# Fewer filler products of TensorE in the norm chains of a Hyena and mLSTM backbone

## The chip, the cores and the metric

The kernel runs on one core of one Trainium2 chip. The metric is the device time of one execution in microseconds (us), as the median of several runs. The profile is of one execution.

## The reference, cut to what matters

The reference is a two-layer backbone over 256 context and 256 latent tokens with 1024 channels. Each layer is a SwiGLU feed-forward part (FFN), a token mixer (Hyena long convolution in layer 0, mLSTM in layer 1) and a second FFN. Each of these six parts starts from a normalised, scaled and shifted copy of the stream `h`, and a seventh norm gives the output:

```python
def rms_norm(x, g):
    y = xf * lax.rsqrt(jnp.mean(xf * xf, axis=-1, keepdims=True) + NORM_EPS)
    return y * g
def ada_pre(h, g, shift, scale):
    return rms_norm(h, g) * (1.0 + scale) + shift
...
h_lat = h_lat + 0.5 * m_lat[2] * swiglu(ada_pre(h_lat, norm_g[l, 0], m_lat[0], m_lat[1]), ...)
h_lat = h_lat + m_lat[5] * y_lat
...
return rms_norm(h_lat, final_g)
```

What is computed does not depend on the products that the change leaves out: nothing reads their result.

## The kernel before, in words

`h` lies in SBUF as eight tiles of 128 channels by 512 tokens. Weights come in 172 blocks of 1 MB through two buffers. ScalarE (ACT) makes the rounded copy `w_hi` (L414), VectorE (DVE) the rest `w_lo` (L807, in two halves in L816), and TensorE (PE) takes each product of a weight and an activation as three products, `w_hi*act_hi`, `w_hi*act_lo` and `w_lo*act_hi` (L1436 to L1438, and L1465 to L1479 in the first two blocks after a norm, `in_pair`). Semaphores order all of it; each engine's program is written out by hand. `w_used` counts weight blocks that TensorE has finished with.

Each of the output projections 0 to 5 (`out_proj`) ends in a call of `chain(o + 1, cols)`: the norm chain. I number the chains 1 to 6. Chains 1 to 4 have all 512 tokens, chains 5 and 6 the 256 latent ones alone; chain 6 is the final norm. A chain runs across three engines:

- TensorE ends the last block. DVE adds each tile of the projection to `h` (L1004), ACT squares it (L425, L428), DVE adds up the squares (L922).
- TensorE sums the squares over the channels with products of one column (`square_sums`, L1514).
- ACT takes the root (L437), DVE the reciprocal (L876) and spreads it on a diagonal (L878).
- TensorE spreads the diagonal over all partitions with one product by ones (`rms_rows`, L1540).
- DVE scales tile by tile (L909), ACT shifts and rounds it to `act_hi` (L449), DVE makes `act_lo` (L895), and TensorE starts `in_pair` (L1465) as soon as the first tile is there. In chain 6 DVE writes the output instead (L902), and two DMAs store it.

While TensorE waits for these steps it is given filler products: `keep_warm(bank, n)` issues n products of the constant tile `cond_pad` with itself, 32 by 256 results in fp32, into a PSUM bank that is free (L1429). In the trace each such product stands as two matmul records. Chain 1 has one filler and otherwise uses the time for real products (`skip_rows`, L1547). Chains 2 to 6 have seven fillers each: three ahead of the sums of squares, two after them, two after the product by ones. The last of the first three (in chain 1 the only one) carries the increment of `w_used` for the last block of the projection; ACT waits for it before it makes `w_hi` of the second block after the norm. The wait for `h_ready` at the head of `chain` makes sure that bank 5 has been read before a filler writes it.

There are 20 more fillers ahead of chain 1 (L1655 to L1713). They are not touched.

Of the kernel before, what the change touches and what calls it, by code (L numbers as in the profile page):

```python
# [73 lines left out]
def build(nc, dram):  # L74
    at, n_vec = column_places()
    with ExitStack() as ctx:
# [12 lines left out]
        def sem(name):  # L89
            return ctx.enter_context(nc.semaphore(name))  # L90
# [112 lines left out]
        w_hi_done, w_lo_done, w_used = sem("w_hi_done"), sem("w_lo_done"), sem("w_used")  # L203
# [1220 lines left out]
        def _(pe):  # L1424
            def keep_warm(bank, n):


                for _ in range(n):
                    mm = pe.matmul(ps[0:32, bank, 0:256], cond_pad[:, 0, :],  # L1429
                                   cond_pad[:].rearrange("p k c -> p (k c)"), start=True, stop=True)  # L1430
                return mm
# [76 lines left out]
            def square_sums(n, cols):  # L1508

                w = (cols.stop - cols.start) // P  # L1510

                def column(t, x, start):
                    c = slice(cols.start + t * P, cols.start + t * P + P)
                    return pe.matmul(ss_col(n, t, 1), x[:, c], col("mean_w"), start=start, stop=not start)  # L1514

                for t in range(w):
                    if w == 4 and t == 0:
                        pe.wait_ge(sq_half, n)
                    elif t == w - 2:
                        pe.wait_ge(sq_ready, 8 * n)  # L1520
                    column(t, sq[:, 1], True)
                pe.wait_ge(sq_added, 6 * n)
                for t in range(w):
                    mm = column(t, sq_sum, False)
                mm.then_inc(ss_done, 1)
# [10 lines left out]
            def rms_rows(n, cols):  # L1536

                pe.wait_ge(diag_ready, n + 1)
                w = (cols.stop - cols.start) // P
                pe.matmul(ps[:, rb_bank(n), cols], ones[:], diag[:, 0:w, :], start=True, stop=True).then_inc(rb_ready, 1)  # L1540

            def skip_rows(u):

                if u == 0:
                    pe.wait_ge(f_dve, DVE_F["skip"])
                for ct in range(4):
                    mm = pe.matmul(ps[:, SKIP_BANKS[u], ct * P:ct * P + P],  # L1547
                                   col("hy_skip", 4 * u + ct).to_broadcast([P, P]), ident[:], start=True, stop=True)
                mm.then_inc(k_skip, 1)

            def chain(n, cols):

                pe.wait_ge(h_ready, 8 * n + 6)
                if n == 1:
                    keep_warm(5, 1).then_inc(w_used, 1)
                    skip_rows(0)
                else:
                    keep_warm(5, 3).then_inc(w_used, 1)
                square_sums(n, cols)
                if n == 1:  # L1560
                    skip_rows(1)
                else:
                    keep_warm(7, 2)
                rms_rows(n, cols)
                if n == 1:
                    skip_rows(2)
                else:
                    keep_warm(7, 2)

            def ffn_in(f, n, cols):  # L1570
                g0 = G_FFN[f]
# [20 lines left out]
            def out_proj(o, cols, between=None):  # L1592
# [53 lines left out]
                for m in range(KT):  # L1646
                    for k in range(2):
                        w, x = ops(k, m)
                        mm = product(ps[:, m, cols], w, x, False, k == 1)
                    mm.then_inc(y_done, 1)  # L1650
                chain(o + 1, cols)


# [449 lines left out]
```

## Time and profile before

| what | us |
|---|---|
| median of 3 runs | 2000.35 |
| the three runs | 1996.58, 2000.86, 2000.35 |
| the profiled execution's own time | 1996.49 |
| its span, first to last instruction | 1994.7 |
| TensorE busy in the span | 1945.8 (98%) |
| VectorE busy | 1214.9 (61%) |
| ScalarE busy | 660.6 (33%) |
| mean granted TensorE clock | 0.987 of full |

The profiled execution's time is its span and 1.8 us around it. A row of the windows view gives a stretch in us from the start of the span, its length, busy time of an engine with its number of instructions, the granted TensorE clock in it (1.00 is 2.4 GHz, 0.50 is 1.2 GHz), the share of time that the DMA engines were busy, and GB/s. A row of the timeline gives start, busy length, engine, line, operation and count, and in square brackets how long the engine was idle before it and what ended that.

### The profile page before, as it was taken

What the parts mean: (1) busy time and instruction counts of PE and PEld (TensorE: products, weight loads), DVE (VectorE), ACT (ScalarE), POOL (GpSimd) and SP (SyncE); (2) the same over time, 40 slices, a digit from 0 to 9 for tenths busy, and PEclk for the clock granted to TensorE, in tenths of its full rate; (3) what the DMA queues carried; (4) which work ended last, traced back from release to release, by engine and by line L of the source; (5) the groups of instructions that cost most, each with busy time, mean ns of one, the idle gap of its engine ahead of it and who ended that gap; (6) DMA issues with size and microseconds to landing.
All of it is one profiled execution on the core that took longest, in us unless ns stands there. A gap on an engine that the chain in (4) does not pass through costs nothing.

```text
span 1994.7 us, 25029 instructions
## 1 busy us (share of the span) xinstructions
PE 1945.8 (98%) x9586; PEld 1583.6 (79%) x9586; DVE 1214.9 (61%) x1608; ACT 660.6 (33%) x679; POOL 85.4 (4%) x169
## 2 busy tenths in 40 slices
PE   8999999999989999999999999999999999899998
PEld 3688888887867778888888788888877768499998
DVE  6976776567568757766755977233273346765455
ACT  5622222243231143221223422222243346444333
POOL 0000100000000000001000010000000010000000
PEclk9899999999999999999999999999999999999999
DMA  9355555422230015555543365222312213044543
GB/s 344 143 188 185 200 186 183 146 86 85 89 116 1 34 64 190 181 197 199 181 157 116 127 201 190 93 105 85 139 64 79 80 64 128 22 140 177 189 174 121
DMA packets 48321, 271.64 MB, mean 136 GB/s; under 512 B 5380, under 2 KB 6148, under 8 KB 24840
## 3 DMA queue, kind: packets, MB, share of 16 engines
q1 hardware_dynamic: 28536, 194.30, 27.5%
q0 software_dynamic: 19728, 76.55, 11.5%
q8 instruction: 39, 0.64, 0.1%
q14 instruction: 18, 0.15, 0.0%
HBM read 269.79 MB, written 1.05 MB: 136 GB/s over the span
## 4 chain that ended last, share of the span: by engine, by line
PE 92%; DVE 5%; ACT 2%; issue 1%; DMA 0%; DVEq 0%; ACTq 0%; SPq 0%
PE ps L1436 25%; PE ps L1437 25%; PE ps L1438 25%; PE ps L1763 2%; PE ps L1844 1%; PE ps L1465 1%; PE ps L1753 1%; PE ps L1466 1%; PE ps L1471 1%; PE ps L1468 1%; PE ps L1929 1%; PE ps L1806 1%; PE ps L1429 1%; PE ps L1479 1%; PE ps L1475 1%
## 5 line engine op out<-in xcount | busy, mean ns | idle before, releaser
L1436 PE MATMUL ps<-act_hi,w_hi 128*128 128x512 f32 (+1 forms) x2560 | 922.0, 360 | 11.0 <-DVE w_lo L807 6.7
L1437 PE MATMUL ps<-act_lo,w_hi 128*128 128x512 f32 (+1 forms) x2560 | 918.7, 359 | 0.0
L1438 PE MATMUL ps<-act_hi,w_lo 128*128 128x512 f32 (+1 forms) x2560 | 918.3, 359 | 0.0
L807 DVE TENSOR_TENSOR w_lo<-w_raw,w_hi 128x2048 fp32r<-128x2048 f32 x167 | 382.6, 2291 | 481.0 <-ACT w_hi L414 480.9
L1436 PEld LDWEIGHTS ps<-act_hi,w_hi 128*128 128x128 f32 x2560 | 485.7, 190 | 87.1 <-DVE w_lo L807 7.5
L1437 PEld LDWEIGHTS ps<-act_lo,w_hi 128*128 128x128 f32 x2560 | 485.9, 190 | 70.7 <-issue 0.5
L1438 PEld LDWEIGHTS ps<-act_hi,w_lo 128*128 128x128 f32 x2560 | 485.8, 190 | 70.6
L414 ACT ACTIVATE w_hi<-w_raw 128x2048 fp32r<-128x2048 f32 x172 | 329.1, 1913 | 620.6 <-PE ps L1438 597.5
L834 DVE SCALAR_TENSOR_TENSOR ada_w<-ada_w,cond_bc 128x1024 f32<-128x1024 f32 x128 | 156.2, 1221 | 0.0
L834 DVE SCALAR_TENSOR_TENSOR ada_prod<-ada_w,cond_bc 128x1024 f32<-128x1024 f32 x128 | 156.1, 1220 | 0.0
L463 ACT ACTIVATE silu_g<-ps 128x1024 f32<-128x1024 f32 (+1 forms) x44 | 40.4, 919 | 295.3 <-PE ps L1438 295.3
L383 POOL DMA_DIRECT2D ada_w<-ada_rows_dram x126 | 66.5, 528 | 1111.0 <-DVE ada_w L834 1106.6
L938 DVE TENSOR_TENSOR scratch<-silu_g,ps 128x1024 f32 (+3 forms) x44 | 47.8, 1087 | 65.2 <-PE ps L1438 65.2
L1763 PE MATMUL ps<-dft_i,zf 128*128 128x256 f32 x256 | 60.8, 398 | 7.3 <-DVE zf L1222 6.8
L1763 PEld LDWEIGHTS ps<-dft_i,zf 128*128 128x128 f32 x256 | 51.1, 201 | 19.1 <-DVE zf L1222 8.0
L1148 DVE TENSOR_SCALAR xc<-pad,vec 128x512 f32<-128x512 f32 x16 | 9.3, 582 | 75.4 <-ACT pad L665 75.4
L1004 DVE SCALAR_TENSOR_TENSOR h<-ps,coef_g,h 128x256 f32<-128x256 f32 x80 | 35.6, 478 | 32.2 <-PE ps L1438 32.2
L964 DVE TENSOR_TENSOR act_lo<-scratch,act_hi 128x1024 fp32r<-128x1024 f32 (+1 forms) x48 | 52.5, 1096 | 1.7 <-ACT act_hi L497 1.7
L497 ACT ACTIVATE act_hi<-scratch 128x1024 fp32r (+3 forms) x48 | 45.2, 945 | 16.5 <-DVE scratch L1233 11.7
L449 ACT ACTIVATE act_hi<-tn,mods 128x256 fp32r<-128x256 f32 x88 | 39.8, 502 | 32.2 <-DVE tn L909 32.2
L625 ACT ACTIVATE pad<-ps,vec 128x512 f32<-128x512 f32 x24 | 15.3, 685 | 95.0 <-PE ps L1438 85.3
L895 DVE SCALAR_TENSOR_TENSOR act_lo<-tn,mods,act_hi 128x256 fp32r<-128x256 f32 x88 | 38.9, 480 | 2.6 <-ACT act_hi L449 2.6
(231 smaller groups left out, 1336.8 us busy)
## 6 DMA issues: line engine op xcount, KB each, us to landing
w_raw<-w_stream_dram SPq DMA_DIRECT2D x172, 1024.0 KB, 4.7
ada_w<-ada_rows_dram POOLq DMA_DIRECT2D x128, 512.0 KB, 3.8
ada_raw<-ada_stream_dram POOLq DMA_DIRECT2D x4, 1024.0 KB, 12.4
ada_in<-ada_stream_dram POOLq DMA_DIRECT2D x4, 1024.0 KB, 16.3
bd<-bd_dram SPq DMA_DIRECT2D x4, 768.0 KB, 6.6
edecay<-log_decay_dram SPq DMA_DIRECT2D x4, 512.0 KB, 10.3
h<-tokens_dram SPq DMA_DIRECT2D x1, 2048.0 KB, 13.0
wg<-wg_dram SPq DMA_DIRECT2D x3, 512.0 KB, 4.5
```

Of the source, the lines that this page charges most:

```text
L383: pool.dma_start(ada_w[:, s], dram["ada_rows"][bass.ds(2 * q + s, 1)].rearrange("a p k -> (a p) k")).then_inc(adaw_loaded[s], 16)
L414: act.activation(w_hi[:, g % 2, :], w_raw[:, g % 2, :], ACT.Copy).then_inc(w_hi_done, 1)
L463: act.activation(silu_g[:, :, cols], ps[:, 0:2, cols], ACT.Silu).then_inc(silu_done, 1)
L497: act.activation(act_hi[:, s:s + 2, cols], src(b, i), ACT.Copy).then_inc(in_hi, 1)
L807: dve.tensor_tensor(w_lo[:, g % 2, :], w_raw[:, g % 2, :], w_hi[:, g % 2, :].bitcast(F32), ALU.subtract).then_inc(w_lo_done, 1)
L834: dve.scalar_tensor_tensor(ada_w[:, s] if cd else ada_prod[:], ada_w[:, s], 1.0, cond_bc[:, cd], ALU.mult, ALU.mult, accum_out=mod_cols[:, ...
L938: dve.tensor_tensor(hidden[:, bass.ds(2 * p + 2 * i, 2), cols], silu_g[:, :, cols], ps[:, 2:4, cols], ALU.mult).then_inc(mul_done, 1)
L964: dve.tensor_tensor(act_lo[:, s:s + 2, cols], src(b, i), act_hi[:, s:s + 2, cols].bitcast(F32), ALU.subtract).then_inc(in_lo, 1)
L1436: pe.matmul(out, wh, xh, start=start, stop=False)
L1437: pe.matmul(out, wh, xl, start=False, stop=False)
L1438: return pe.matmul(out, wl, xh, start=False, stop=stop)
L1763: mm = pe.matmul(ps[:, inv_bank(st) + ct // 2, ct % 2 * 256:ct % 2 * 256 + 256], zf[:, (st + 1) % 2, q, ct * P:ct * P + P], dft_i[:, q // ...
```

## The change

Chains 2 to 6 keep one filler of seven: the one that carries the increment of `w_used`. It is issued as the first now, where it was the third. Chain 1 and all fillers ahead of it stay. The order of all other instructions, and all waits, stay.

```diff
                     keep_warm(5, 1).then_inc(w_used, 1)
                     skip_rows(0)
                 else:
-                    keep_warm(5, 3).then_inc(w_used, 1)
+                    keep_warm(5, 1).then_inc(w_used, 1)
                 square_sums(n, cols)
                 if n == 1:
                     skip_rows(1)
-                else:
-                    keep_warm(7, 2)
                 rms_rows(n, cols)
                 if n == 1:
                     skip_rows(2)
-                else:
-                    keep_warm(7, 2)
```

## Rows read from the trace of the kernel before

**Rows 1.** The page: chain that ended last by engine; costliest group of instructions.

```profile
PE 92%; DVE 5%; ACT 2%; issue 1%; DMA 0%; DVEq 0%; ACTq 0%; SPq 0%
L1436 PE MATMUL ps<-act_hi,w_hi 128*128 128x512 f32 (+1 forms) x2560 | 922.0, 360 | 11.0 <-DVE w_lo L807 6.7
```

**Rows 2.** View of line L1429: count: min/median/max ns, first and last start.

```profile
L1429 PE MATMUL ps<-cond_pad x112: 379/379/636, 4.3 to 1989.0; 128*32 128x256 f32 x112
```

**Rows 3.** Timeline of chain 2, its last DVE update of `h` to `in_pair`.

```profile
733.16 1.48 PE L1429 MATMUL ps<-cond_pad 128*32 128x256 f32 x6
...
733.99 0.42 ACT L425 ACTIVATE sq<-h 128x256 f32<-128x256 f32 x1 [0.36 <-DVE h L1004]
...
734.58 1.05 PE L1514 MATMUL ps<-vec,sq 128*128 128x1 f32 x8
...
736.45 1.05 PE L1429 MATMUL ps<-cond_pad 128*32 128x256 f32 x4
...
736.72 1.90 ACT L414 ACTIVATE w_hi<-w_raw 128x2048 fp32r<-128x2048 f32 x1
...
737.07 0.69 DVE L878 TENSOR_TENSOR diag<-ident,cols 128x512 f32<-128x512 f32 x1
...
737.82 1.12 PE L1540 MATMUL ps<-diag,ones 128*128 128x512 f32 x2 [0.31 <-DVE diag L878]
...
738.87 1.05 PE L1429 MATMUL ps<-cond_pad 128*32 128x256 f32 x4
738.98 1.65 DVE L909 SCALAR_TENSOR_TENSOR tn<-h,coef_a,ps 128x256 f32<-128x256 f32 x4
...
741.00 0.47 PE L1465 MATMUL ps<-act_hi,w_hi 128*128 128x512 f32 x1 [1.08 <-ACT act_hi L449]
```

**Rows 4.** Windows of TensorE over chains 1 (four), 2, 5 and 6.

```profile
434.00:435.50 1.50, 1.50 (x11) 1.00 0.00 0
435.50:438.90 3.40, 3.10 (x27) 1.00 0.00 0
439.00:442.30 3.30, 3.22 (x10) 0.50 0.37 97
442.50:446.00 3.50, 3.43 (x15) 1.00 0.45 190
733.10:741.00 7.90, 6.51 (x34) 1.00 0.10 17
...
1787.20:1793.10 5.90, 5.27 (x27) 1.00 0.00 0
1984.20:1989.40 5.20, 5.11 (x25) 1.00 0.01 2
```

**Rows 5.** The chain that ended last, around chain 2: start, us, what.

```profile
733.24 1.41 PE ps L1429 x6
734.65 1.89 PE ps L1514 x16
```

**Rows 6.** Timeline of chain 6: its product by ones, its last fillers, the output.

```profile
1987.66 0.70 PE L1540 MATMUL ps<-diag,ones 128*128 128x256 f32 x2
...
1988.29 1.05 PE L1429 MATMUL ps<-cond_pad 128*32 128x256 f32 x4
1988.40 3.22 DVE L902 SCALAR_TENSOR_TENSOR out_sb<-h,vec,ps 128x256 f32<-128x256 f32 x8 [0.79 <-PE ps L1540]
```

**Rows 7.** Timeline of chain 1 on TensorE, cut to four rows.

```profile
434.00 0.62 PE L1429 MATMUL ps<-cond_pad 128*32 128x256 f32 x2
...
438.68 1.83 PE L1540 MATMUL ps<-diag,ones 128*128 128x512 f32 x2 [0.30 <-DVE diag L878]
...
440.31 1.91 PE L1547 MATMUL ps<-ident,vec 128*128 128x128 f32 x8
...
442.57 0.47 PE L1465 MATMUL ps<-act_hi,w_hi 128*128 128x512 f32 x1 [0.35 <-ACT act_hi L449]
```

**Rows 8.** Windows of TensorE around two other gaps, at 476 and at 1734 us.

```profile
476.40:479.90 3.50, 0.00 (x1) 1.00 0.00 0
479.95:486.70 6.75, 6.15 (x15) 0.50 0.44 155
486.80:493.55 6.75, 6.75 (x32) 1.00 0.45 155
...
1734.56:1737.80 3.24, 0.00 (x1) 1.00 0.00 0
```

**Rows 9.** Waits of TensorE from 1793 to 1830 us: who, for whom, total, times, longest.

```profile
PE ps L1436 <- DVE w_lo L807: 0.6, 1, 0.6
```

## The prediction, made before the changed kernel ran

> **What bounds the kernel now.** I read the page first. The chain of work that ended last is 92% TensorE, and the costliest group alone is 922.0 us of products [rows 1]. So almost every microsecond in which TensorE does its weight products more slowly is a microsecond of the end time. The fillers stand with 112 records in the view of their line [rows 2]. Each product is two records, so that is 56 products: 20 ahead of chain 1, 1 in chain 1, 35 in chains 2 to 6. The change removes six in each of five chains: 30 products, 60 records.
>
> Next I read the timeline of one chain [rows 3]. The reader should see that TensorE waits three times there: for squares from ACT, for the diagonal from DVE, and for the first `act_hi` tile. The fillers lie in these waits. Then I read the windows for the granted clock [rows 4]: over the whole of chains 2, 5 and 6 it is 1.00, and in chain 1, which has one filler, it falls to 0.50 from 439.0 to 442.3 us. Chains 3 and 4 repeat chain 2 within 0.1 us, also at 1.00. The question of this change is what the clock does once the fillers are gone.
>
> **The change part by part.**
>
> *Time of the fillers themselves: 0.* Removing work from a wait gives nothing back if something else ends the wait. Ahead of the sums of squares, L425 on ACT ends at 733.99 + 0.42 = 734.41 and L1514 starts at 734.58; in that time the fillers (733.16 for 1.48 us) are just draining [rows 3]. The chain view puts them on the path, with 1.41 us [rows 5], because they stand just ahead on the engine. If that were right, leaving out two of three would give 2/3 of 1.41 = 0.94 us in each of five chains, 4.7 us in all. I take 0, because the start fits the end of L425. The two fillers after the sums end at 736.45 + 1.05 = 737.50, and the product by ones starts at 737.82, after the diagonal (737.07 + 0.69 = 737.76). The last two end at 739.92, and `in_pair` starts at 741.00, on `act_hi`. In chain 6 the last two run beside the output, which DVE had already begun to wait for [rows 6]. All 0.
>
> *The earlier increment of `w_used`: 0.* Two fillers less ahead of it bring it about 0.9 us earlier. Only ACT's L414 waits for it there, and in program order L414 stands behind the root. It starts at 736.72, two microseconds after the increment has come [rows 3]; what hides it is the root. No queue is passed, and no wait is added.
>
> *The clock.* Chain 1 shows what happens with one filler. From 434.0 to 438.9 us TensorE ran one filler, 16 records of L1547 and 16 of one-column products; it was busy 1.50 + 3.10 of 4.90 us, and at 439.0 the clock was 0.50 [rows 4]. After the change chains 2 to 6 have over the same steps one filler and the one-column products alone: less than a chain that fell. So I expect all of them to fall. Chain 1 also shows the way back: after the product by ones it still had eight records of L1547, 1.91 us [rows 7], which kept TensorE busy (3.22 of 3.30 us) at the low clock, and at 442.5 the clock was 1.00 again, in time for `in_pair`. Chains 2 to 5 have nothing there. TensorE is idle from the end of the product by ones, 737.82 + 1.12 = 738.94, to 741.00 [rows 3], and it must win the clock back with the weight products themselves, at half speed.
>
> *The price, bounded from both sides.* The lower end is chain 1. Its product by ones took 1.83 us instead of 1.12, which is 0.71 us on the path [rows 3, 7]. The whole chain from the first filler to `in_pair` took 442.57 - 434.00 = 8.57 us against 741.00 - 733.16 = 7.84, so 0.73: the same. The upper end adds a gap that was followed by dense products: after the gap at 476 us the clock was 0.50 from 479.95 to 486.7, in which TensorE was busy 6.15 us [rows 8]. The row behind it has 32 records in the same 6.75 us against 15, so half of the 6.15 us is lost: 3.1 us. Both together are 3.8 us for a chain. If all is unknown, a gain is excluded: a lower clock makes nothing faster. Where between 0.7 and 3.8 a chain lands depends on when in the chain the clock falls and comes back, which differs from chain to chain. The case is nearer to the second row, as the recovery is by dense products, but not all of the low stretch need lie behind the start of `in_pair`, and not every product by ones need fall in it. I take the middle, 2.25 us, for chains 2, 3 and 4: 6.75 us.
>
> *Chain 5* has half as many tokens; its product by ones is 0.70 us, as the one of chain 6 [rows 6], so at half clock I add 0.4. The dense part costs up to 3.1, and TensorE later waits 0.6 us for `w_lo` [rows 9], which a slower start would hide. So 0 + 0.4 to 0.4 + 3.1 - 0.6 = 2.9 us, and I take the middle, 1.6. *Chain 6* has no dense products behind it, and its product by ones, at 1987.66, comes only 3.5 us after its first filler [rows 4, 6], so it is often still at the full clock: 0 to 0.4, I take 0.1. After chains 2 to 4 no wait of TensorE stands that could hide the loss.
>
> *The sum* is 6.75 + 1.6 + 0.1 = 8.4 us. Against the profiled execution's 1996.49 that makes 2004.9. That execution lies 3.9 us below the median of the runs shown; the four times known (1996.49, 1996.58, 2000.35, 2000.86) have a mean of 1998.6, and a median of new runs should lie about 8.4 above that: **2007.0 us**.
>
> A rule that speaks for another sum: here a chain in which TensorE was never idle for more than 0.35 us fell [rows 4, 7], while 3.24 us without a product at 1734.56 left the clock at 1.00 [rows 8]. The Trainium skill, in "TensorE: Matmul & The Clock Gate", section "HAM oscillation — how this bites in real kernels", ties the fall to gaps in which TensorE is idle. By that rule the changed chains, whose longest idle time is shorter than the gap at 1734.56, would hold the clock, and the sum would be 0. By the rows it is 8.4, since chain 1 contradicts the rule.
>
> **The rivals.**
>
> *The clock holds (0.09): not slower.* The mechanism is idle time and not the kind of work. Its place is TensorE's longest idle time after the change, 738.94 to 741.00, which is 2.06 us. For it speaks that the gap of 3.24 us at 1734.56 cost no clock; against it, chain 1. It decides if idle times of about 2 us do not bring the fall. The rule of the Trainium skill named above is this mechanism. Sum 0: time 1996.5 to 2000.9, within 0.2%. Should it hold in some chains only, the sum shrinks by 2.25 for each.
>
> *The clock falls but is back before `in_pair` (0.05).* Each chain would then cost what chain 1 cost: 3 x 0.7 + 0.4 = 2.5 us, so 2001.1. Against it: with no product between 738.94 and 741.00 nothing shows TensorE busy there.
>
> *The fillers were on the path (0.04).* The chain view says so [rows 5]; the clock would have to hold too. Price: a gain of up to 4.7 us, 1994. Against it stands the end of L425 just ahead of L1514 [rows 3].
>
> *The forecast (0.82):* at least three of chains 2 to 5 fall and come back only behind the start of `in_pair`.
>
> **How the numbers follow.** The four chains fall independently, so their ends do not all meet: I take 5 to 12 us for the sum rather than 2.1 to 14.7. With a low base of 1996.5 and a high one of 2000.4 the range is 2001.5 to 2012. It leaves out the rivals (0.18 together, of which the second reaches its edge) and little else. What a measurement of this kernel can tell from no change is about 0.2%, 4 us. Slower by more than that: nearly all of the forecast, 0.78. Within it: the clock that holds, the early recovery, and the small end of the forecast, 0.17. Faster: 0.05.
>
> **What would show each step.** Right: the windows of chains 2 to 5 show a granted clock of 0.50 from somewhere in the chain to 2 to 6 us behind the start of `in_pair`; weight products there stand 0.43 us apart instead of 0.23; some products by ones take about 1.8 us; L425 to L1514 and the diagonal to L1540 keep their distances; the mean clock falls from 0.987 by about 0.005. Wrong: a clock of 1.00 through chains 2 to 5, or L1514 starting earlier after the last block than now, or a wait on `w_lo` later in the FFN that shrinks by as much as the clock costs.

## The result, and where the time went

The changed kernel takes 2012.19 us as the median of 7 runs (2006.18 to 2016.23), the kernel before 2000.86 (7 runs, 1996.58 to 2005.03). The ratio is 1.0058, with a 95% interval of 1.0044 to 1.0072: by it the change costs 11.6 us, between 8.8 and 14.4 (the two medians lie 11.3 apart). The profiled execution took 2014.09 us, its span is 2012.2 and its mean granted clock 0.975, against 0.987.

The profile page of the changed kernel shows nearly the same busy times as before. The chain that ended last has 90% TensorE instead of 92, and the costliest group, L1436, is at 922.1 us instead of 922.0 [rows 1]. A part of the loss shows in the smaller group L1465, the first weight products behind a chain:

```profile
L1465 PE MATMUL ps<-act_hi,w_hi 128*128 128x512 f32 (+1 forms) x96 | 39.8, 417 | 8.6 <-ACT act_hi L449 8.6
```

Before, its mean was 379 ns, and it waited 4.1 us for `act_hi`. The page does not say where that happens. The windows of TensorE over the chains do. The columns are those of [rows 4].

```profile
738.74:740.80 2.06, 1.95 (x16) 1.00 0.00 0
740.83:746.10 5.27, 2.08 (x2) 0.50 0.36 110
746.11:751.07 4.96, 4.96 (x12) 0.50 0.23 96
751.10:756.00 4.90, 4.90 (x23) 1.00 0.00 0
...
1112.90:1116.20 3.30, 1.32 (x2) 0.50 0.40 112
1116.28:1119.70 3.42, 3.42 (x8) 0.50 0.45 192
...
1485.79:1491.70 5.91, 5.91 (x14) 0.50 0.18 72
...
1808.26:1812.60 4.34, 4.34 (x20) 0.50 0.58 236
```

The first four are chain 2: the sums of squares still run at 1.00, the product by ones at 0.50, and `in_pair` starts at 746.11 and does twelve records in 4.96 us at 0.50, where the same length at 1.00 holds 23. The others are chain 3, and the first products of `in_pair` after chains 4 and 5. Before, none of these stretches was below 1.00: chains 2, 5 and 6 are in [rows 4], chains 3 and 4 stood at 1.00 too, and these are the windows behind chains 2 to 5 in the kernel before:

```profile
741.00:751.00 10.00, 10.00 (x44) 1.00 0.22 93
1108.30:1119.70 11.40, 11.37 (x50) 1.00 0.19 80
1475.40:1491.70 16.30, 16.30 (x72) 1.00 0.22 78
1793.10:1812.00 18.90, 18.32 (x151) 1.00 0.51 175
```

After the change the weight products run at the low clock for 4.96, 3.42, 5.91 and 4.34 us, and about half of this is lost. From the fall to the return the low clock lasts about 10.2 us in chains 2 and 4 and about 6.8 us in chains 3 and 5:

```profile
740.85:751.05 10.20, 7.02 (x14) 0.50 0.30 104
1112.90:1119.70 6.80, 4.74 (x10) 0.50 0.43 154
1481.55:1491.75 10.20, 8.03 (x16) 0.50 0.28 104
1805.80:1812.60 6.80, 5.54 (x22) 0.50 0.41 155
```

The timeline of chain 3 has the steps of [rows 3]:

```profile
1107.96 0.62 PE L1429 MATMUL ps<-cond_pad 128*32 128x256 f32 x2
...
1108.78 0.42 ACT L425 ACTIVATE sq<-h 128x256 f32<-128x256 f32 x1 [0.36 <-DVE h L1004]
...
1109.25 1.05 PE L1514 MATMUL ps<-vec,sq 128*128 128x1 f32 x8 [0.67 <-ACT sq L425]
...
1112.49 1.73 PE L1540 MATMUL ps<-diag,ones 128*128 128x512 f32 x2 [1.29 <-DVE diag L878]
...
1114.26 1.66 DVE L909 SCALAR_TENSOR_TENSOR tn<-h,coef_a,ps 128x256 f32<-128x256 f32 x4 [0.69 <-PE ps L1540]
...
1116.28 0.77 PE L1465 MATMUL ps<-act_hi,w_hi 128*128 128x512 f32 x1 [2.06 <-ACT act_hi L449]
```

The product by ones takes 1.73 us instead of 1.12, and DVE now waits for it. In chains 2 and 4 TensorE is busy with it for 2.08 and 2.07 us. To give each chain one price I take, from the timelines, the time from the start of the last weight product ahead of the chain (L1438) to the start of the last product of `in_pair` (L1479); in chain 6 it ends at the start of the first output (L902). Before, these are 29.77, 29.79, 29.81, 17.50 and 4.43 us.

| chain | 2 | 3 | 4 | 5 | 6 | sum |
|---|---|---|---|---|---|---|
| added by the change, us | 3.16 | 2.10 | 3.62 | 2.17 | 0.48 | 11.5 |
| predicted | 2.25 | 2.25 | 2.25 | 1.6 | 0.1 | 8.4 |

The two chains with the longer low stretch cost most. The sum of 11.5 us is as much as the measured difference. This one profile is 17.6 us longer than that of before; the other 6 us lie elsewhere, and 4.4 of them ahead of chain 1 (its last weight product starts at 438.11 instead of 433.68), where both kernels have the same program.

One profile is one execution, and stretches that the change does not touch can go either way. Chain 1, whose program is the same in all the kernels of this document, fell to 0.50 before [rows 4] and held the clock in the changed kernel's profile:

```profile
441.00:446.20 5.20, 3.83 (x26) 1.00 0.15 32
```

Over the nine profiles taken for this document it fell in five and held in four. For the chains with one filler or with all seven there was no such doubt: chains 2 to 6 fell in both profiles of the changed kernel, ten of ten, and held, ten of ten, in the two kernels that keep all seven (before, and `more_gaps` below).

### The profile page after: what moved, and what is told of

It reads as the page before. It is cut to its first block, busy times and chain, and to the rows that moved or that the text cites. A ratio compares the mean times of both kernels' runs of the same rounds, so it can differ in the third digit from the quotient of the medians.

```text
span 2012.2 us, 24909 instructions
## 1 busy us (share of the span) xinstructions
PE 1948.7 (97%) x9526; PEld 1588.1 (79%) x9526; DVE 1214.6 (60%) x1608; ACT 660.7 (33%) x679; POOL 85.4 (4%) x169
## 3 DMA queue, kind: packets, MB, share of 16 engines
q0 software_dynamic: 19728, 76.55, 11.3%
HBM read 269.79 MB, written 1.05 MB: 135 GB/s over the span
## 4 chain that ended last, share of the span: by engine, by line
PE 90%; DVE 6%; ACT 2%; issue 1%; DMA 0%; DVEq 0%; ACTq 0%; SPq 0%
PE ps L1436 24%; PE ps L1438 24%; PE ps L1437 24%; PE ps L1759 2%; PE ps L1840 1%; PE ps L1465 1%; PE ps L1466 1%; PE ps L1749 1%; PE ps L1468 1%; PE ps L1471 1%; PE ps L1925 1%; PE ps L1802 1%; PE ps L1475 1%; PE ps L1479 1%; PE ps L1679 1%
## 5 line engine op out<-in xcount | busy, mean ns | idle before, releaser
L1436 PE MATMUL ps<-act_hi,w_hi 128*128 128x512 f32 (+1 forms) x2560 | 922.1, 360 | 11.0 <-DVE w_lo L807 6.7
L1438 PE MATMUL ps<-act_hi,w_lo 128*128 128x512 f32 (+1 forms) x2560 | 918.9, 359 | 0.0
L1436 PEld LDWEIGHTS ps<-act_hi,w_hi 128*128 128x128 f32 x2560 | 486.3, 190 | 86.6 <-DVE w_lo L807 7.5
L1438 PEld LDWEIGHTS ps<-act_hi,w_lo 128*128 128x128 f32 x2560 | 486.1, 190 | 71.0
L414 ACT ACTIVATE w_hi<-w_raw 128x2048 fp32r<-128x2048 f32 x172 | 329.1, 1913 | 626.1 <-PE ps L1438 597.6
L1465 PE MATMUL ps<-act_hi,w_hi 128*128 128x512 f32 (+1 forms) x96 | 39.8, 417 | 8.6 <-ACT act_hi L449 8.6
```

What stands on the lines that cost most here:

```text
L414: act.activation(w_hi[:, g % 2, :], w_raw[:, g % 2, :], ACT.Copy).then_inc(w_hi_done, 1)
L1436: pe.matmul(out, wh, xh, start=start, stop=False)
L1438: return pe.matmul(out, wl, xh, start=False, stop=stop)
L1465: pe.matmul(ps[:, t, cols], wh[0][:, k, c[t]], act_hi[:, k, cols], start=k == 0, stop=False)
```

## The experiments

I set two theories against each other. **A**: the clock falls in these chains because too few products of many columns are left in them, whatever the busy time says. **B** is that it falls because TensorE is idle in the waits. That is the rule of the Trainium skill, "TensorE: Matmul & The Clock Gate", section "HAM oscillation — how this bites in real kernels". All kernels but `more_gaps` differ from the changed kernel in the fillers of chains 2 to 6 alone, if at all. In the diffs, lines of chain 1 and bare `else:` lines are left out.

**Busy, but narrow.** `narrow` issues products of one column:

```diff
+            def narrow(bank, n):
+                for _ in range(n):
+                    pe.matmul(ps[:, bank, 0:1], ident[:], col("mean_w"), start=True, stop=True)
...
                     keep_warm(5, 1).then_inc(w_used, 1)
+                    narrow(5, 4)
                 square_sums(n, cols)
+                    narrow(7, 4)
                 rms_rows(n, cols)
+                    narrow(7, 4)
```

> The changed kernel, with each filler of 256 columns that it left out replaced by two products of one column with 128x128 weights, about the same busy time (some 0.48 us against 0.43). Theory A (the clock is held by products that stream many columns, whatever the busy time says): the granted clock falls to 0.50 in chains 2 to 5 as in the changed kernel, and the time is 8 to 14 us above the kernel before. Theory B (the clock falls because TensorE is idle in the waits): its longest idle time in a chain is now as short as before the change, the clock stays at 1.00 in chains 2 to 5, and the time is within 2 us of before.

Measured: 2011.9 us (4 runs), ratio 1.0055 [1.0037, 1.0074]: 11 us slower, just as the changed kernel. Chain 2 on TensorE, first as timeline and then in windows (the helper moves the lines: L1436 is the narrow filler, L1519 the sums, L1545 the product by ones, L1470 the first weight product):

```profile
737.44 0.62 PE L1429 MATMUL ps<-cond_pad 128*32 128x256 f32 x2
737.99 1.05 PE L1436 MATMUL ps<-vec,ident 128*128 128x1 f32 x8
738.90 1.03 PE L1519 MATMUL ps<-vec,sq 128*128 128x1 f32 x8
739.79 1.03 PE L1519 MATMUL ps<-vec,sq_sum 128*128 128x1 f32 x8
740.69 1.75 PE L1436 MATMUL ps<-vec,ident 128*128 128x1 f32 x8
742.30 2.05 PE L1545 MATMUL ps<-diag,ones 128*128 128x512 f32 x2
744.14 1.71 PE L1436 MATMUL ps<-vec,ident 128*128 128x1 f32 x8
746.41 0.76 PE L1470 MATMUL ps<-act_hi,w_hi 128*128 128x512 f32 x1 [0.56 <-ACT act_hi L449]
```

```profile
737.00:740.80 3.80, 3.80 (x31) 1.00 0.00 0
740.90:746.40 5.50, 4.95 (x18) 0.50 0.34 113
746.41:751.00 4.59, 4.59 (x11) 0.50 0.21 89
```

TensorE is busy for 3.80 of 3.80 us and the clock falls all the same. Its longest idle time in the chain is 0.56 us, shorter than the 1.08 us with which the kernel before kept the clock [rows 3]. That settles it against B, if idle means that no product is under way. The clock fell in chains 3 to 6 too. Chains 2 to 5 add 3.3, 3.9, 2.3 and 2.3 us by the measure of the table. For A it shows that the narrow products did not do the work of the wide ones. The two kinds differ in more than their columns, though: a filler has 32 columns of weights and other data, a narrow product has 128. Which of this counts was not tested.

**Which fillers matter.** Four kernels give back some of the groups; I name them by the fillers in the three places. Before is 3, 2, 2; the changed kernel is 1, 0, 0.

```diff
-                    keep_warm(5, 1).then_inc(w_used, 1)
+                    keep_warm(5, 3).then_inc(w_used, 1)
```

is `first_only` (3, 0, 0). The others put `keep_warm(7, 2)` back ahead of `rms_rows` (`middle_only`: 1, 2, 0), behind it (`last_only`: 1, 0, 2) or at both (`one_two_two`: 1, 2, 2).

> Three fillers ahead of the sums of squares, none behind them. Theory A: from the sums to the first weight product, 6.4 us, there is only the product by ones, so the clock falls in chains 2 to 5 nearly as in the changed kernel: 7 to 12 us above before. Theory B: the idle times of 1.3 and 2.06 us behind the sums stay as they were, so also 7 to 12 us. It tells where the fillers matter, not why.

> One filler ahead of the sums, two between the sums and the product by ones, none behind it. Theory A: the stretch without wide products is cut in two, and the second fillers join the product by ones; the clock falls in some chains only, 1 to 7 us above before. Theory B: the idle time of 2.06 us ahead of the first weight product is the longest and stays, so the time is that of the changed kernel, 8 to 14 us above.

> One filler ahead of the sums, none between, two behind the product by ones. Theory A: the clock falls as in the changed kernel around the sums, but the last fillers keep TensorE busy at half clock up to the first weight product, as L1547 does in chain 1, and bring the clock back sooner: per chain 0.7 to 2 us instead of 2 to 3.6, in all 3 to 7 us above before. Theory B: the longest idle time is now 1.3 us, nearly the 1.08 of before, so the clock holds and the time is within 2 us.

> Only the two fillers ahead of the sums of squares are left out, those behind stay: 10 of the 30. Theory A: the stretch without a wide product is 734.6 less some 0.9 us earlier to 736.4, not much longer than before; the clock holds in most chains, 0 to 2 us above before, and L1514 starts 0.1 us earlier after the last weight product, as in the changed kernel. If each filler counts the same, 10 of 30 give a third of 11.6 us: about 4 us above.

| fillers | median, us | ratio to before | chains 2 to 5, added in the profile, us |
|---|---|---|---|
| 1, 0, 0 | 2012.19 | 1.0058 [1.0044, 1.0072] | 3.2, 2.1, 3.6, 2.2 |
| 3, 0, 0 | 2007.36 | 1.0032 [1.0022, 1.0043] | 2.8, 2.2, 2.2, 2.2 |
| 1, 2, 0 | 2007.95 | 1.0034 [1.0020, 1.0047] | 2.8, 1.5, 1.5, 2.1 |
| 1, 0, 2 | 2003.16 | 1.0013 [1.0002, 1.0024] | 1.6, 1.4, 1.5, 1.0 |
| 1, 2, 2 | 2002.63 | 1.0012 [1.0003, 1.0022] | 1.1, 1.0, 0.8, 1.0 |

(The median of before beside them is 2000.86 for the first, 2001.41 for the next three and 2000.61 for the last.) The chains of the one profile add more than the medians differ, by 1 to 3 us in the last four rows. What sets this off elsewhere is open, so I compare these kernels by their medians and use the profiles for the mechanism.

`first_only` came out at 6.4 us [4.4, 8.6], under its 7 to 12 but for the end of the interval. `middle_only`, with 6.8 us [4.0, 9.4], is within A's 1 to 7 and just under B's 8 to 14, and its interval reaches into both, so it does not decide. A's mechanism was not right there either: I expected a fall in some chains only, and the clock fell in each of chains 2 to 5, in chain 2 twice. In chains 3 and 4 it fell only behind the start of `in_pair`, and they paid less (1.5 us). `last_only`, with 2.6 us [0.4, 4.8], lies under A's 3 to 7, and its time alone would not exclude B; its windows do:

```profile
736.80:740.40 3.60, 2.91 (x20) 1.00 0.00 0
740.50:745.70 5.20, 3.92 (x6) 0.50 0.28 95
745.80:747.30 1.50, 1.50 (x4) 0.50 0.82 344
747.40:751.00 3.60, 3.60 (x18) 1.00 0.00 0
```

The clock falls in chain 2 (as in 3 to 5), but only 1.5 us of weight products run at the low level, instead of 4.96. The last fillers don't keep the clock here; with them it comes back sooner. That is what I expected of them, with a smaller remainder. In `one_two_two` I was wrong on the mechanism: I expected the clock to hold in most chains, and it fell in each of chains 2 to 5. Its chain 2:

```profile
738.60:742.20 3.60, 2.93 (x21) 1.00 0.00 0
742.40:745.70 3.30, 3.30 (x6) 0.50 0.00 0
745.80:748.00 2.20, 1.12 (x6) 1.00 0.80 309
747.94:751.00 3.06, 3.06 (x14) 1.00 0.28 115
```

It is back at 1.00 before the first weight product at 747.94, so that the chain pays for its product by ones and no more. Chains 3 and 4 do the same. This is the prediction's second rival, at somewhat more than its price (0.8 to 1.1 us a chain instead of 0.7), in another kernel. Chain 5 still runs its first weight products low. So the two fillers ahead of the sums are worth 2.4 us [0.6, 4.4], though they save no wait. Between `last_only` and `one_two_two`, which differ in the middle fillers, the medians show no difference that counts (2.6 and 2.4 us above before).

**The changed kernel once more.**

> The changed kernel once more, for a second profile. Theory A: the clock falls in chains 2 to 5 again, but elsewhere in each chain and for other lengths, so that a chain costs 2 to 4 us with another distribution over the chains; the 4.4 us that the first profile lost ahead of chain 1, where the programs are the same, are chance and should differ. Time 8 to 14 us above before.

Measured: 2009.9 us (4 runs), 1.0048 [1.0033, 1.0063], which is 9.6 us slower and within the expected 8 to 14. Chain 2 again, on TensorE:

```profile
734.20:737.90 3.70, 2.92 (x20) 1.00 0.00 0
738.10:743.10 5.00, 2.08 (x2) 0.50 0.32 95
743.22:748.20 4.98, 4.98 (x12) 0.50 0.24 102
```

Chains 2 to 5 add 3.25, 2.10, 3.63 and 2.19 us: the first profile's 3.16, 2.10, 3.62, 2.17 within 0.1 us. I had expected another distribution, and was wrong. Whether this is a property of the program or of two like executions stays open; the chains of `narrow`, which have nearly the same length, give another one. The time ahead of chain 1 did differ, as expected: its last weight product starts at 435.72, against 438.11 in the first profile and 433.68 before.

**More fillers instead of fewer.** The same remedy should pay in waits that have no filler. A and B both say so; this run tests the remedy and not the theories. [rows 8] show one such wait at 476 us. To place a filler there the edit takes the first turn out of the loop; the order of the other products stays.

```diff
             skip_rows(3)
-            with pe.Fori(0, 5) as i:
-                hy_in(2, i)
-                hy_in(3, i)
+            hy_in(2)
+            pe.wait_ge(pad_ready, 4)
+            keep_warm(2, 8)
+            hy_in(3)
+            with pe.Fori(0, 4) as i:
+                hy_in(4, i)
+                hy_in(5, i)
...
             turn(0)
+            keep_warm(4, 6)
...
+                if st == 1:
+                    keep_warm(4, 8)
+                elif st == 8:
+                    keep_warm(6, 4)
                 if st > 0:
                     inverse(st - 1)
...
                     head_matrix(j // 2)
+                    if j == 0:
+                        keep_warm(4, 5)
```

> The kernel before, all its fillers kept, with 31 more fillers in five other waits in which or behind which the clock fell before: 8 in the wait at 476 us, 6 at 583, 8 at 597, 4 at 678, 5 at 1498, each time a little less than the wait is long. Theory A: the low stretches behind these waits (6.2 us of weight products at 480, 2.5 and 1.9 us too much in L1763 at 602 and 681, about 1.5 us at 1501) go, and the time is 4 to 8 us under before. Theory B (idle time alone brings the fall) expects the same here, as these waits are idle. A rival to both: fillers there delay the engine's next work or contend with it, 0 to 3 us above before.

Measured: 1990.69 us (6 runs) against 2000.61, ratio 0.9954 [0.9940, 0.9968]: 9.2 us faster than before, between 6.4 and 12, where I had expected 4 to 8. Two of the places in the timeline of TensorE:

```profile
478.67 3.64 PE L1429 MATMUL ps<-cond_pad 128*32 128x256 f32 x16
482.99 0.47 PE L1436 MATMUL ps<-act_hi,w_hi 128*128 128x512 f32 x1 [0.68 <-DVE w_lo L807]
...
595.11 3.64 PE L1429 MATMUL ps<-cond_pad 128*32 128x256 f32 x16
599.75 2.42 PE L1767 MATMUL ps<-dft_i,zf 128*128 128x256 f32 x10 [1.00 <-DVE zf L1222]
```

And the windows, without the fillers (the kernel before, around the same places):

```profile
583.00:602.00 19.00, 11.04 (x33) 0.84 0.39 150
601.65:611.00 9.35, 9.35 (x33) 0.76 0.01 2
680.84:689.70 8.86, 8.86 (x33) 0.81 0.53 189
```

with them:

```profile
478.00:484.00 6.00, 5.32 (x25) 1.00 0.04 4
...
590.00:600.00 10.00, 8.60 (x34) 1.00 0.29 107
600.00:611.00 11.00, 11.00 (x48) 1.00 0.00 0
680.00:690.00 10.00, 10.00 (x46) 1.00 0.26 102
```

The first inverse transform (32 records, L1763 there and L1767 here) takes 7.17 us instead of 9.41, the last one 7.17 instead of 8.86. From the start of `in_pair` behind chain 1 to the last weight product ahead of chain 2 the profile before has 732.85 - 442.57 = 290.3 us and this one 727.03 - 444.88 = 282.1: 8.1 us less, nearly all of the 9.2. That compares single executions: the low stretch at 480 us lasts 6.8 us in the profile before and about 3.4 us in the seven others that have no filler there, so with another profile this part would come out smaller. The fillers at 1498 us show no gain: from the `in_pair` behind chain 4 to chain 5 both have the same within 0.4 us, though the low stretch at 1500 us is gone.

## Why the prediction was wrong

The way, the mechanism and the places were right; the size was not. I forecast 2007.0 and a range up to 2012.0, and the median is 2012.19. The step that failed is the price of the full chains, 2.25 us each, which measured 3.16, 2.10 and 3.62. A smaller part is the base.

- **The fillers' own time, 0**: nearly right. L425 to L1514 shrank from 0.17 us [rows 3] to 1109.25 - (1108.78 + 0.42) = 0.05. Here TensorE starts sooner after the wait with no filler draining, a gain of 0.12 us in each of chains 2 to 4, not the 0.94 that the chain view [rows 5] would have given. The prediction had named an earlier L1514 as a sign of being wrong; it came, at this small size.
- **The increment of `w_used`, 0**: right. L414 still starts directly behind the root.
- **The clock falls in chains 2 to 5**: right in all four and in chain 6, in both profiles. The reading of chain 1 as the nearest case carried it. That was in part luck: chain 1 fell in only five of the nine profiles, so another profile of before might have shown it at 1.00.
- **"I take the middle, 2.25 us, for chains 2, 3 and 4"**: this step failed. They cost 3.16, 2.10 and 3.62, 8.9 us instead of 6.75; only chain 3 came near the middle. I argued that "not every product by ones need fall in" the low stretch, but it did in all three, in chain 3 for most of its length; and it cost 0.61 to 0.95 us (from its start to `in_pair` chains 2 and 3 take 4.13 and 3.79 us, where [rows 3] have 3.18), while I had taken the 0.71 of chain 1 as its most, where only a part of it ran at the low clock. The weight products ran low for 3.42 to 5.91 us, a loss of 1.7 to 3.0, in chains 2 and 4 near the upper row's 3.1 and not midway from 0. The whole low stretch was 10.2 us there, longer than the 6.75 us of that row, so the upper end was not a bound either. I had written that the case "is nearer to the second row" and then taken the middle.
- **Chain 5, 1.6 us**: 2.17. The wait for `w_lo` that I let hide 0.6 us was not shortened at all. It stands in the waits of the changed kernel, 1808 to 1830 us, as in [rows 9]:

```profile
PE ps L1436 <- DVE w_lo L807: 0.6, 1, 0.6
```

  That wait follows TensorE's own progress rather than the time on DVE, so a later TensorE seems only to move it. What drives it I did not test.
- **Chain 6, 0.1 us**: 0.48. Its product by ones took 1.22 us instead of 0.70 [rows 6].
- **The mean clock**: it fell from 0.987 to 0.975, by 0.012 and not by about 0.005. The low stretches of chains 2 to 5, 34.0 us together, make 34.0 x 0.5 / 2012.2 = 0.008 of it.
- **The base**: I added the sum to 1998.6, the mean of four times. The seven runs of before have a median of 2000.86, which is 2.3 us of the 5.2 by which I missed; the terms above are 3.1 (the two overshoot by 0.2).
- **The range**: the sum of 11.5 us is inside its 5 to 12, near the end. 12 us over the high base of 2000.4 is 2012.4, and I wrote 2012; with the sum done right the median of 2012.19 would have been just inside, which would have been no better forecast. By saying that the ends of the chains "do not all meet" I cut it close: no full chain came near the lower end of 0.7. That they share a condition, no wide products ahead of `in_pair`, may be why; so they are not independent.
- **The rival in which the clock holds**: excluded for this kernel by the changed profile, and its mechanism by `narrow`. The rule of the Trainium skill ("TensorE: Matmul & The Clock Gate", section "HAM oscillation — how this bites in real kernels") speaks of idle gaps and does not cover a TensorE that is busy with narrow products; by `narrow`, where the longest idle time in chain 2 was 0.56 us, the trace disagrees with it as a complete account.
- **The gap at 1734.56 that kept the clock** [rows 8]: no property of the gap. The same wait, 3.25 us long in every profile, is followed by a stretch at 1.00 in five of the nine and by one at 0.50 in four, here in `more_gaps`, where it ends at 1730.87:

```profile
1727.65:1730.85 3.20, 0.00 (x0) 1.00 0.00 0
1731.70:1735.05 3.35, 3.35 (x18) 0.50 0.00 0
```

  So neither this gap nor chain 1 could tell, from one profile, what idle time does. What decides in a single execution is open.

## What to carry to other kernels

A filler product is judged by what it does to the granted clock, not by its place in a wait: read the windows view over the wait and over the dense work behind it. Products of 256 columns held it here; products of one column kept TensorE as busy and were worth nothing. Where only some can be had, those directly ahead of the dense work were worth most here, since the fallen clock was back sooner. Do not judge by a single profile whether a wait costs the clock: two unchanged places went one way in five profiles and the other way in four. Then look for waits of a few microseconds that have none, with dense work on the critical path behind them: four such waits gave 8 us here.

## What the runs showed of the hardware that I had not expected

- Fillers at the low clock take nearly twice as long, and by that fill more of the wait: the two behind the product by ones take 1.05 us before [rows 3] and 1.92 us in chain 2 of `last_only`, up to 0.21 us ahead of the first weight product.
- Weight products that start at the low clock may stay there for up to 5.91 us of full work (1485.79 to 1491.70), longer than the 4.1 us before it at 0.50 in which TensorE had nothing but the product by ones.
- The change costs nearly the same in each of chains 2 to 5 in two executions (3.16, 2.10, 3.62, 2.17 and 3.25, 2.10, 3.63, 2.19 us), while stretches with the same program, ahead of chain 1, differ by 2.0 and 4.4 us from before.
